# A ring of ten weight units instead of eight, residual rows parked in memory, and separate buffers for the last tiles, in a transformer block with a mixture of experts

## The chip, the cores and the metric

The kernel runs on one core of one Trainium2 chip. Its time is the device time of one execution in microseconds (us), the median of three runs. All work of the core is done by five engines with a program each: PE (matmul), DVE (vector), ACT (scalar activation), POOL (general) and SP (which here only issues transfers), and by 16 DMA engines that they share. Programs wait for each other by semaphores.

## The reference

One block over 1024 tokens of width 1024, all in fp32. A projection feeds two mixers (a chunked mLSTM and a sparse attention), their outputs go through `w_out`, and then come the residual and a mixture of experts, on which this change works:

```python
y = jnp.concatenate([y_m, y_n], axis=-1) @ w_out[l]
x = x + g_m * rms_norm(y, norm_mix_post[l])              # these are the "residual rows", x2 in the kernel
h = rms_norm(x, norm_ffn_pre[l]) * (1.0 + sc_f) + sh_f
y = hier_moe(h, router_grp_w[l], ..., expert_w1[l], expert_w3[l], expert_w2[l])
x = x + g_f * rms_norm(y, norm_ffn_post[l])

# hier_moe: each token picks one of 4 groups, then 2 of its 8 experts; for each block of rows of one expert
xb = hf[toks]
hb = jax.nn.silu(xb @ w1[ei]) * (xb @ w3[ei])            # w1, w3: 1024 x 512
return (hb @ w2[ei]) * gts[:, None]                      # w2: 512 x 1024
```

There are 32 experts, each with three weight matrices of 2048 KB, and 2048 pairs of a token and an expert.

## The kernel before

Everything on chip lies in one array, `arena`, of 53200 words in each of 128 partitions, which the program cuts into regions that later stages use again. The stages that matter here are the last four.

**Stage E** (from about 786 us) runs over 8 tiles of 128 tokens. For each tile PE turns the mixers' output and multiplies it with `w_out`, ACT and DVE normalise it, DVE adds the rows of `x` (loaded into `xt[t % 2]`) and writes the sum into `x2[:, t, :]`, which stays on chip in the region `QT` until the very end. The tile, normalised once more (`xn2`), is stored to `d_xn` in memory. After the last tile the router runs on DVE: it counts the rows of each expert, ranks the experts by that count and writes `row_tok` and `expert_at`, the tables that say which tokens and which expert stand at which place. The semaphore `table_ready` marks this.

**Places.** The experts are given 32 places. Places 0 to 2 belong to experts 0, 1 and 2 whatever their count, so that their weights can be loaded before the router is done; the others follow by falling count. The capacity falls with the place (`CAP_STEPS`): 128 rows at places 0 to 6, 96 at 7 to 13, 64 at 14 to 26, 32 at 27 to 31. What doesn't fit goes to extra blocks of 128 rows behind the 32 steps (`over_block`); with these inputs there is one.

**The expert stage** handles the places in the order of the list `ORDER`, one in each step q. PE does in a step: "up" (rows times w1 and w3, `f_up`), the turning of the next step's rows (`f_turn`), "down" of the step before (hidden times w2, `f_down`) and the turning of the hidden rows (`f_turn_hidden`). POOL gathers the rows of step q from `d_xn` two steps ahead, ACT and DVE do the gating, DVE copies the results out and ACT stores them to `d_y`. SP loads the weights: one unit is one matrix of 2048 KB, `(1, q)`, `(3, q)` or `(2, q)` for w1, w3 or w2 of step q, and there are eight slots for units (`SLOT`). `LOADS` is the order of the loads, the unit number v goes to slot v % 8, and it may start when unit v - 8 has been used (`slot_free`): w1 after the first half of "up" (semaphore `up_half`), w3 after the second (`up_done`), w2 after "down" (`down_done`). SP takes its instructions in order, so a load that waits holds back all that follow. The first eight units belong to places 0 to 2 and need no table.

**The final stage** starts when all results are stored (`stage_f`). POOL gathers for each of 8 tiles of 128 tokens the two experts' rows from `d_y` into `y1` and `y2`, ACT scales the first, DVE adds the second, ACT sums the squares, DVE normalises, scales and adds `x2[:, t, :]`, and SP stores the tile to `out`. `y1` and `y2` have four buffers each (`NG = 4`): from tile 4 on, POOL waits until the tile four before has been stored.

Of the kernel before, what the change touches and what calls it, by code (L numbers as in the profile page):

```python
# [85 lines left out]
def weight_loads():  # L86
# [7 lines left out]
LOADS = weight_loads()  # L94
# [65 lines left out]
def build(nc, d, out):  # L160
    JOB = job_list()
    ITEMS = ring_items(d)
    with ExitStack() as ctx:
# [162 lines left out]
        x2 = view(QT, NT, D)  # L326
# [47 lines left out]
        NG = 4  # L374
        y1 = [view(SLOT[0] + D * i, D) for i in range(NG)]
        y2 = [view(SLOT[0] + D * (NG + i), D) for i in range(NG)]
        junk_g = view(SLOT[0] + 2 * NG * D, D)
# [15 lines left out]
        w_in = [sem(f"w_in{j}") for j in range(8)]  # L393
# [11 lines left out]
        y_in = [sem(f"y_in{i}") for i in range(4)]  # L405
        g_scaled, g_added, g_sq, g_sqrt, g_done = (sem(n) for n in ("g_scaled", "g_added", "g_sq", "g_sqrt", "g_done"))
        out_stored = [sem(f"out_stored{i}") for i in range(4)]
# [143 lines left out]
        def _(sp):  # L551
# [101 lines left out]

            sp.wait_ge(x_sq, NT)
            sp.wait_ge(psum_ready, JOB[("xT2", NT - 1, 1)] + 1)
            for s in range(2):
                sp.wait_ge(xn_stored[s], 16 * NT // 2)
            load_static(5)
            sp.wait_ge(stage_end["E"], 4)
            sp.wait_ge(table_ready, 1)  # L660
            load_static(6)
            for v in range(8, len(LOADS)):
                n, q = LOADS[v]
                e = q
                if q >= 3:
                    e = sp.value_load(expert_at[ORDER[q]:ORDER[q] + 1, 0:1], min_val=0, max_val=NE - 1)
                slot_free(v - 8)
                load_weight(v % 8, n, e)

            def load_over(i, s):  # L670
# [18 lines left out]
            for t in range(NT):
                sp.wait_ge(g_done, t + 1)  # L690
                sp.dma_start(out[t * P:(t + 1) * P, :], y1[t % NG]).then_inc(out_stored[t % NG], 16)
            for s in range(NG):
                sp.wait_ge(out_stored[s], 16 * NT // NG)

        @block.gpsimd
        def _(pool):
# [103 lines left out]
            for t in range(NT):  # L800
                if t >= NG:
                    pool.wait_ge(out_stored[t % NG], 16 * (t // NG))
                for k, y in enumerate((y1, y2)):
                    pool.indirect_dma_start(y[t % NG], None, d_y,
                                            bass.IndirectOffsetOnAxis(ap=dest[:, k, t:t + 1], axis=0)).then_inc(y_in[t % NG], 16)
# [1281 lines left out]
```

## Time and profile before

| | |
|---|---|
| Time, median of 3 runs | 1637.09 us (1636.88 to 1637.14) |
| Time of the profiled execution | 1636.61 us |
| Its span | 1634.8 us |
| Granted TensorE clock, mean over the span | 0.924 of full |
| PE busy | 1360.1 us (83%) |
| DVE busy | 632.0 us (39%) |
| ACT busy | 385.1 us (24%) |
| Moved by DMA | 323.01 MB, mean 198 GB/s |

All times in the rows are microseconds from the start of the span unless marked ns. The profiled execution took 1.8 us more than its span, in what lies around it. "Busy" of PE counts matmuls, also those at the lower clock. In a row of the timeline the first number is the start and the second the duration of a merged group of instructions (merging can take in short waits between them); the bracket at its end is idle time of that engine just before, and what ended it. "DMA share" is the mean busy share of the 16 DMA engines.

### The profile page before, as it was taken

How to read it: one execution, taken by the hardware profiler on the slowest of the kernel's cores; microseconds unless marked ns; L12 is line 12 of the kernel's file. 1: busy time of each engine (PE TensorE's matmuls, PEld its weight loads, DVE VectorE, ACT ScalarE, POOL GpSimd, SP SyncE). 2: the span in 40 equal slices, each digit the busy share in tenths (PEclk: the TensorE clock that was granted, in tenths of full speed). 3: DMA queues.
4: the chain of work that ended last, by engine and by line, in shares of the span. 5: the costliest groups of instructions: out<-in, count | busy, mean ns of one | idle time of the engine just before them, and what ended most of it. 6: DMA issues, size and time to landing. Idle time of an engine off the chain costs nothing.

```text
span 1634.8 us, 17119 instructions
## 1 busy us (share of the span) xinstructions
PE 1360.1 (83%) x6271; PEld 693.1 (42%) x6271; DVE 632.0 (39%) x1400; ACT 385.1 (24%) x873; POOL 77.7 (5%) x109
## 2 busy tenths in 40 slices
PE   2899999999866889998899838999797897898730
PEld 2744444444664444444455424444343343343310
DVE  5626324502065666665333371223122122122216
ACT  2233311101185565544133300000000000000013
POOL 0000000000103000000000000000000000000012
PEclk8899999999997999999999958999899899999975
DMA  9612222202502930000421256699999999999835
GB/s 336 134 51 78 86 81 103 70 33 103 205 2 60 293 117 1 1 1 1 180 78 52 73 207 233 223 403 401 405 405 389 410 397 392 411 389 408 369 116 205
DMA packets 107771, 323.01 MB, mean 198 GB/s; under 512 B 26012, under 2 KB 50216, under 8 KB 99112
## 3 DMA queue, kind: packets, MB, share of 16 engines
q1 hardware_dynamic: 95192, 291.48, 47.6%
q0 software_dynamic: 5712, 19.42, 3.7%
q10 hardware_dynamic: 6784, 11.02, 1.8%
q8 instruction: 51, 0.84, 0.2%
q14 instruction: 32, 0.26, 0.0%
HBM read 283.59 MB, written 38.30 MB: 197 GB/s over the span
## 4 chain that ended last, share of the span: by engine, by line
PE 36%; DMA 13%; DVE 5%; issue 2%; SPq 2%; ACT 2%; POOL 0%; DVEq 0%; ACTq 0%; POOLq 0%
DMA arena<-expert_w 10%; PE ps L1444 7%; PE ps L1433 7%; PE ps L1393 6%; PE ps L1483 5%; PE ps L1299 2%; SPq L623 2%; PE ps L1316 2%; PE ps L1336 2%; ACT arena L980 1%; PE ps L1423 1%; DVE arena L1988 1%; PE ps L1378 1%; DMA d_y<-arena 1%; DMA arena<-d_y,arena 1%
## 5 line engine op out<-in xcount | busy, mean ns | idle before, releaser
L1444 PE MATMUL ps<-arena 128*32 128x256 f32 (+1 forms) x1408 | 203.5, 515 | 49.4 <-DMA arena<-expert_w 48.6
L1154 PE MATMUL ps<-arena 128*128 128x512 f32 x512 | 221.0, 593 | 0.0
L1483 PE MATMUL ps<-arena 128*32 128x256 f32 (+2 forms) x832 | 152.7, 498 | 6.6 <-issue 3.9
L1154 PEld LDWEIGHTS ps<-arena 128*128 128x128 f32 x512 | 97.1, 190 | 119.5 <-issue 119.4
L1444 PEld LDWEIGHTS ps<-arena 128*32 128x32 f32 (+1 forms) x1408 | 78.5, 131 | 160.6 <-issue 147.5
L1161 PE MATMUL ps<-arena 128*128 128x512 f32 (+1 forms) x384 | 142.0, 530 | 1.2 <-ACT arena L825 1.2
L1433 PE MATMUL ps<-arena 128*128 128x512 f32 x256 | 116.1, 612 | 12.9 <-DVE arena L1988 12.9
L1393 PE MATMUL ps<-arena 128*128 128x512 f32 x256 | 112.7, 593 | 0.1
L980 ACT ACTIVATE arena<-arena 128x640 f32<-128x640 f32 (+7 forms) x128 | 92.7, 726 | 59.2 <-DVE arena L1790 59.2
L1161 PEld LDWEIGHTS ps<-arena 128*128 128x128 f32 x384 | 72.5, 189 | 68.7 <-issue 62.0
L1046 ACT ACTIVATE arena<-ps 64x512 f32<-64x512 f32 x20 | 11.8, 589 | 365.3 <-PE ps L1444 365.3
L1316 PE MATMUL ps<-arena 128*128 128x128 f32 x528 | 80.2, 286 | 21.2 <-ACT arena L980 9.2
L1999 DVE TENSOR_TENSOR arena<-arena,ps 64x512 f32<-64x512 f32 x20 | 13.8, 690 | 214.5 <-ACT arena L1046 115.2
L1790 DVE CUSTOM_DVE_ANT_0 arena<-ps,arena 128x640 f32<-128x640 f32 (+7 forms) x128 | 84.5, 704 | 31.4 <-PE ps L1299 29.2
L1483 PEld LDWEIGHTS ps<-arena 128*32 128x32 f32 (+2 forms) x832 | 56.6, 132 | 82.1 <-issue 73.0
L1316 PEld LDWEIGHTS ps<-arena 128*128 128x128 f32 x528 | 58.6, 142 | 77.4 <-issue 25.3
L1299 PE MATMUL ps<-arena 64*128 64x512 f32 (+3 forms) x384 | 73.7, 499 | 14.6 <-DVEq L530 8.5
L1433 PEld LDWEIGHTS ps<-arena 128*128 128x128 f32 x256 | 49.5, 196 | 74.2 <-issue 66.3
L1988 DVE TENSOR_SCALAR arena<-ps,arena 128x64 f32<-128x64 f32 (+3 forms) x264 | 74.4, 356 | 10.0 <-PE ps L1423 8.0
L775 POOL DMA_INDIRECT arena<-d_xn,arena x32 | 30.0, 937 | 933.3 <-PE ps L1423 479.0
L1336 PE MATMUL ps<-arena 128*64 128x512 f32 x264 | 72.0, 625 | 0.0
L1393 PEld LDWEIGHTS ps<-arena 128*128 128x128 f32 x256 | 47.3, 189 | 54.7 <-issue 54.7
(318 smaller groups left out, 1312.4 us busy)
## 6 DMA issues: line engine op xcount, KB each, us to landing
arena<-expert_w SPq DMA_DIRECT2D x99, 2048.0 KB, 33.0
arena<-ada_w SPq DMA_DIRECT2D x12, 2048.0 KB, 9.2
d_y<-arena SPq DMA_DIRECT2D x24, 512.0 KB, 5.9
arena<-x SPq DMA_DIRECT2D x16, 512.0 KB, 4.0
arena<-w_in SPq DMA_DIRECT2D x4, 2048.0 KB, 12.9
d_y<-arena ACTq DMA_DIRECT2D x40, 128.0 KB, 7.9
arena<-w_out SPq DMA_DIRECT2D x2, 2048.0 KB, 14.0
d_xn<-arena SPq DMA_DIRECT2D x8, 512.0 KB, 2.6
```

What stands on the lines that cost most here:

```text
L980: nc.scalar.activation(p_, p_, ACT.Exp, scale=-1.0, bias=nmax[:, (u + g) % 8:(u + g) % 8 + 1], accum_out=sums[:, t % 2, "csw".index(kind), ...
L1154: last = nc.tensor.matmul(b, w(k), hT[:, k, 512 * c:512 * c + 512], start=(k == 0), stop=(k == KT - 1))
L1161: last = nc.tensor.matmul(b[:, 0:width], hT[:, k, P * t:P * t + P], w[:, k, at_col:at_col + width], start=(k == 0), stop=(k == KT - 1))
L1299: last = nc.tensor.matmul(b, qT[half, h, at_t], src[half, first + at_:first + at_ + w], start=True, stop=True)
L1316: last = nc.tensor.transpose(b[g][:, P * h:P * h + P], probs[kind][g][h][:, P * i:P * i + P], ident)
L1336: last = nc.tensor.matmul(ps[HD * g:HD * g + HD, 6, :], vv[:, blocks[i], P * k + HD * g:P * k + HD * g + HD], probs_T[q % 2][g], start=(i ...
L1393: last = nc.tensor.matmul(b, yT[t % 2][:, k, :], w[:, k, :], start=(k == 0), stop=(k == KT - 1))
L1433: last = nc.tensor.matmul(ps[:, 2 + n, :], xgT[s][:, k, :], w_up[slots[n]][:, k, :], start=(k == 0), stop=(k == KT - 1))
L1444: last = nc.tensor.matmul(ps[width * j:width * j + width, 2 if width == 64 else 3, 0:span], xgT[s][:, k, lo:lo + width], w_up[slots[n]][:, ...
L1483: last = nc.tensor.matmul(dst, hid_T[s][:, at_:at_ + width], w_down[slot][:, k, span * j:span * j + span], start=(k == 0), stop=(k == 3))
L1790: V.tensor_tensor_reduce(probs[kind][g][h][:, 0:n], ps[:, b0:b0 + 2, :].rearrange("p a n -> p (a n)")[:, 0:n] if n > 512 else ps[:, b0, 0: ...
L1988: last = V.tensor_scalar(xgT[s][:, k, 0:rows], turned_at(k, rows), scale_f[:, k:k + 1], shift_f[:, k:k + 1], ALU.mult, ALU.add)
```

## The change

Four things are changed, and they hang together by the room on chip.

- The residual rows no longer stay on chip. DVE adds in place in `xt[t % 2]`, SP stores that tile to a new memory tensor `d_x2`, and loads the next `x` tile into the buffer only when the store has landed. The region `QT` becomes two weight slots. All of `d_x2` is read back (two transfers of four tiles each) after the last "up" of the 32 steps, into the two slots of that step's w1 and w3.
- The ring has ten slots. Unit v (from 10 on) takes the slot of unit v - 10 in the order in which units are *used* (`USES`), not loaded.
- `ORDER` is changed: the three fixed experts (places 0, 1, 2) stand at steps 0, 2 and 4, and places 27, 28 and 29, of 32 rows, stand between them. All nine units of the fixed experts are loaded before the table is ready: five at the start of stage E, two at its next to last tile, two at its end.
- In the final stage each tile has its own `y1` and `y2`, and POOL no longer waits for stores of `out`.

```diff
-SLOT = [0, 4096, 8192, MQT, MKT, MKT + 4096, MKT + 8192, YM]
-ORDER = [0, 1, 2, 14, 27, 7, 3, 15, 8, 16, 28, 17, 4, 9, 18, 19, 29, 10, 20, 5, 21, 11, 30, 22, 23, 12, 6, 24, 25, 13, 26, 31]
+SLOT = [0, 4096, 8192, QT, QT + 4096, MQT, YM, MKT, MKT + 4096, MKT + 8192]
+NS = 10
+ORDER = [0, 27, 1, 28, 2, 29, 14, 7, 3, 30, 15, 8, 16, 17, 4, 9, 18, 19, 10, 20, 5, 21, 11, 22, 23, 12, 6, 24, 25, 13, 26, 31]
...
-    loads = [(n, q) for q in range(2) for n in (1, 3)] + [(2, 0), (2, 1), (1, 2), (3, 2)]
-    for q in range(3, NE):
-        loads += [(1, q), (3, q), (2, q - 1)]
-    return loads + [(2, NE - 1)]
+def weight_uses():
+    uses = []
+    for q in range(NE):
+        uses += [(1, q), (3, q)] + [(2, q - 1)] * (q > 0)
+    return uses + [(2, NE - 1)]
+USES = weight_uses()
+EARLY = [(n, q) for q in range(NE) if ORDER[q] < 3 for n in (1, 3, 2)]
+LOADS = EARLY + [u for u in USES if u not in EARLY]
+SLOT_OF, FILLS, fills = {}, {}, [0] * NS
+for v, u in enumerate(LOADS):
+    SLOT_OF[u] = v if v < NS else SLOT_OF[USES[v - NS]]
...
-        x2 = view(QT, NT, D)
-        NG = 4
+        NG = NT
+        x2_slots = [SLOT_OF[(n, NE - 1)] for n in (1, 3)]
+        x2_back = [view(SLOT[j], 4, D) for j in x2_slots]
...
-            for v in range(3):
+            for v in range(5):
                 load_static(v)
             for t in range(NT):
                 sp.wait_ge(x2_done, t + 1)
-                if t + 2 < NT:
-                    sp.dma_start(xt[t % 2], d["x"][(t + 2) * P:(t + 3) * P, :]).then_inc(xt_in[t % 2], 16)
-                if t == NT - 1:
-                    sp.wait_ge(psum_ready, JOB[("out", NT - 1, 1)] + 1)
-                    for v in (3, 4, 7):
-                        load_static(v)
+                sp.dma_start(d_x2[t * P:(t + 1) * P, :], xt[t % 2]).then_inc(x2_stored[t % 2], 16)
                 sp.wait_ge(xn2_done, t + 1)
                 sp.dma_start(d_xn[t * P:(t + 1) * P, :], xn2[t % 2]).then_inc(xn_stored[t % 2], 16)
+                if t + 2 < NT:
+                    sp.wait_ge(x2_stored[t % 2], 16 * (t // 2) + 16)
+                    sp.dma_start(xt[t % 2], d["x"][(t + 2) * P:(t + 3) * P, :]).then_inc(xt_in[t % 2], 16)
+                if t == NT - 2:
+                    sp.wait_ge(psum_ready, JOB[("yT", NT - 1, 1)] + 1)
+                    load_static(5)
+                    load_static(6)
...
+            for v in range(NS - 1, len(LOADS)):
                 n, q = LOADS[v]
+                if v >= NS:
+                    slot_free(USES[v - NS])
...
+            sp.wait_ge(up_done, NE)
+            for a in range(2):
+                sp.dma_start(x2_back[a], d_x2[4 * P * a:4 * P * a + 4 * P, :].rearrange("(t p) n -> p t n", p=P)).then_inc(x2_in, 16)
...
             for t in range(NT):
-                if t >= NG:
-                    pool.wait_ge(out_stored[t % NG], 16 * (t // NG))
...
-                V.tensor_tensor(x2[:, t, :], y_row, xt[t % 2], ALU.add).then_inc(x2_done, 1)
+                V.tensor_tensor(xt[t % 2], xt[t % 2], y_row, ALU.add).then_inc(x2_done, 1)
...
+            dve.wait_ge(x2_in, 32)
             add_experts(0)
```

PE at the start of the expert stage, before. L1433 is "up" of 128 rows, L1423 the turning of the next rows (the second number of its shape is how many), L1456 the turning of the hidden rows, L1483 "down", L1444 "up" of fewer rows.

```order
L1423 MATMUL ps<-arena 128x128 x8
L1433 MATMUL ps<-arena 128x512 x16
L1423 MATMUL ps<-arena 128x128 x8
L1456 MATMUL ps<-arena 128x128 x4
L1433 MATMUL ps<-arena 128x512 x16
L1423 MATMUL ps<-arena 128x128 x8
L1483 MATMUL ps<-arena 128x512 x8
L1456 MATMUL ps<-arena 128x128 x4
L1433 MATMUL ps<-arena 128x512 x16
```

The same place after the change, where these lines are L1451, L1441, L1474 and L1479, L1501 and L1462:

```order
L1441 MATMUL ps<-arena 128x128 x8
L1451 MATMUL ps<-arena 128x512 x16
L1441 MATMUL ps<-arena 128x32 x8
L1474 MATMUL ps<-arena 128x128 x4
L1462 MATMUL ps<-arena 32x256 x32
L1441 MATMUL ps<-arena 128x128 x8
L1501 MATMUL ps<-arena 128x512 x8
L1479 MATMUL ps<-arena 128x64 x2
L1451 MATMUL ps<-arena 128x512 x16
L1441 MATMUL ps<-arena 128x32 x8
L1501 MATMUL ps<-arena 32x256 x16
```

Three steps of 128 rows stood in a row; now a step of 32 rows follows each of them.

SP from the seventh tile of stage E to the first loads with the table, before. L646 loads `x`, L652 stores `xn2`, L623 loads w1 or w3 and L621 w2, L666 reads `expert_at`.

```order
L646 DMA arena<-x 128x1024 [waits x2_done]
L652 DMA d_xn<-arena 128x1024 [waits xn2_done]
L652 DMA d_xn<-arena 128x1024 [waits xn2_done,x2_done]
L623 DMA arena<-expert_w 128x4096 [waits psum_ready,x2_done]
L621 DMA arena<-expert_w 128x4x1024
L623 DMA arena<-expert_w 128x4096
L652 DMA d_xn<-arena 128x1024 [waits xn2_done]
L621 DMA arena<-expert_w 128x4x1024 [waits xn_stored0,xn_stored1,psum_ready,x_sq]
L623 DMA arena<-expert_w 128x4096 [waits table_ready,stage_endE]
L666 TENSOR_LOAD arena
```

And after the change (L660 stores `d_x2`, printed `d_x`; L662 stores `xn2`, L665 loads `x`, L637 and L635 load weights, L683 reads `expert_at`):

```order
L660 DMA d_x<-arena 128x1024 [waits x2_done]
L662 DMA d_xn<-arena 128x1024 [waits xn2_done]
L665 DMA arena<-x 128x1024 [waits x2_stored1]
L660 DMA d_x<-arena 128x1024 [waits x2_done]
L662 DMA d_xn<-arena 128x1024 [waits xn2_done]
L635 DMA arena<-expert_w 128x4x1024 [waits psum_ready]
L637 DMA arena<-expert_w 128x4096
L660 DMA d_x<-arena 128x1024 [waits x2_done]
L662 DMA d_xn<-arena 128x1024 [waits xn2_done]
L637 DMA arena<-expert_w 128x4096 [waits x2_stored1,x2_stored0,psum_ready]
L635 DMA arena<-expert_w 128x4x1024 [waits xn_stored1,xn_stored0]
L683 TENSOR_LOAD arena [waits table_ready,stage_endE]
```

A load of `x` now stands behind two stores and a wait, and no weight load but the tenth waits for the table.

## Rows read from the trace of the kernel before

**Rows 1.** The page: GB/s in the 40 equal slices of the span.
```profile
GB/s 336 134 51 78 86 81 103 70 33 103 205 2 60 293 117 1 1 1 1 180 78 52 73 207 233 223 403 401 405 405 389 410 397 392 411 389 408 369 116 205
```
**Rows 2.** Windows: stretch, its length, busy of each engine, PEclk, DMA share, GB/s.
```profile
955.00:977.00 22.00, 7.05 (x32) 6.90 (x32) 19.08 (x69) 0.00 (x0) 1.85 (x1) 0.50 0.27 96
977.00:1010.00 33.00, 23.76 (x61) 11.78 (x62) 6.88 (x20) 1.88 (x2) 2.83 (x3) 0.78 0.67 240
1010.00:1060.00 50.00, 50.00 (x155) 22.80 (x155) 11.26 (x27) 1.78 (x3) 2.68 (x3) 1.00 0.61 210
1060.00:1549.00 489.00, 425.67 (x2637) 186.21 (x2636) 118.49 (x323) 17.34 (x35) 23.80 (x28) 0.94 1.01 401
...
986.00:1537.00 551.00, 491.65 (x2828) 216.19 (x2828) 130.63 (x351) 21.01 (x40) 27.39 (x31) 0.95 0.96 376
```
**Rows 3.** Waits of PE from 1062 to 1545 us.
```profile
PE ps L1444 <- DMA arena<-expert_w: 48.6, 13, 7.7
```
**Rows 4.** Timeline of PE, expert stage, one row for each kind of work.
```profile
986.08 16.59 PE L1433 MATMUL ps<-arena 128*128 128x512 f32 x32 [2.81 <-DVE arena L1988]
...
1021.03 7.04 PE L1483 MATMUL ps<-arena 128*128 128x512 f32 x16
...
1028.35 13.92 PE L1433 MATMUL ps<-arena 128*128 128x512 f32 x32
...
1066.22 3.66 PE L1444 MATMUL ps<-arena 128*32 128x256 f32 x64
...
1086.43 1.94 PE L1483 MATMUL ps<-arena 128*32 128x256 f32 x32
```
**Rows 5.** Timeline of SP, first loads with the table.
```profile
996.01 7.18 SPq L623 DMA_DIRECT2D arena<-expert_w  x2
```
**Rows 6.** L623, all its loads.
```profile
DMA to landing us min/median/max: 8.1/33.6/41.2
```
**Rows 7.** The page: DMA issues, count, KB each, median us to landing.
```profile
arena<-expert_w SPq DMA_DIRECT2D x99, 2048.0 KB, 33.0
...
arena<-x SPq DMA_DIRECT2D x16, 512.0 KB, 4.0
...
d_xn<-arena SPq DMA_DIRECT2D x8, 512.0 KB, 2.6
```
**Rows 8.** Timeline, the end of the expert stage.
```profile
1535.44 1.93 PE L1483 MATMUL ps<-arena 128*32 128x256 f32 x32 [1.87 <-DMA arena<-expert_w]
...
1540.46 0.42 DVE L2017 COPY arena<-ps 128x256 f32<-128x256 f32 x1 [6.22 <-DMA d_y<-arena]
...
1544.66 15.49 PE L1433 MATMUL ps<-arena 128*128 128x512 f32 x32 [6.05 <-DVE arena L1988]
...
1571.14 1.18 ACTq L1058 DMA_DIRECT2D d_y<-arena  x2
...
1578.98 0.94 POOL L804 DMA_INDIRECT arena<-d_y,arena  x1 [70.76 <-DVEq L2048]
```
**Rows 9.** Windows, the final stage.
```profile
1579.00:1635.00 56.00, 0.00 (x0) 0.00 (x0) 31.22 (x32) 21.12 (x33) 17.99 (x16) 0.50 0.64 225
```
**Rows 10.** Waits in the final stage.
```profile
POOL arena L804 <- DMA out<-arena: 19.2, 4, 9.9
```
**Rows 11.** Timeline of the final stage, POOL, DVE and SP.
```profile
1580.23 0.94 POOL L804 DMA_INDIRECT arena<-d_y,arena  x1 [0.30 <-issue]
...
1594.01 1.23 DVE L2065 TENSOR_TENSOR arena<-arena 128x1024 f32<-128x1024 f32 x1
...
1630.41 1.23 DVE L2065 TENSOR_TENSOR arena<-arena 128x1024 f32<-128x1024 f32 x1
```
**Rows 12.** Timeline of SP, stage E.
```profile
832.24 0.33 SPq L646 DMA_DIRECT2D arena<-x  x1
834.90 0.33 SPq L652 DMA_DIRECT2D d_xn<-arena  x1
849.50 0.33 SPq L646 DMA_DIRECT2D arena<-x  x1
```

More of the change, by code:

```diff
@@ L83 @@
 STEP_ROWS = [rows_of(place) for place in ORDER]
-def weight_loads():
-    loads = [(n, q) for q in range(2) for n in (1, 3)] + [(2, 0), (2, 1), (1, 2), (3, 2)]
-    for q in range(3, NE):
-        loads += [(1, q), (3, q), (2, q - 1)]
-    return loads + [(2, NE - 1)]
-LOADS = weight_loads()
+def weight_uses():
[9 more added lines that the diff above has]
+    SLOT_OF[u] = v if v < NS else SLOT_OF[USES[v - NS]]
+    fills[SLOT_OF[u]] += 1
+    FILLS[u] = 16 * fills[SLOT_OF[u]]
+OVER_SLOT = [[SLOT_OF[USES[len(LOADS) - NS + 3 * s + j]] for j in range(3)] for s in range(2)]
+OVER_FILLS = [[16 * fills[j] for j in slots] for slots in OVER_SLOT]
 STORES = [0, 0]
@@ L372, in build @@
         assert small[0] <= late_end
-        NG = 4
-        y1 = [view(SLOT[0] + D * i, D) for i in range(NG)]
-        y2 = [view(SLOT[0] + D * (NG + i), D) for i in range(NG)]
-        junk_g = view(SLOT[0] + 2 * NG * D, D)
+        NG = NT
+        x2_slots = [SLOT_OF[(n, NE - 1)] for n in (1, 3)]
+        x2_back = [view(SLOT[j], 4, D) for j in x2_slots]
+        y_slots = [SLOT[j] for j in range(NS) if j not in x2_slots]
+        y1 = [view(y_slots[i // 4] + D * (i % 4), D) for i in range(NG)]
+        y2 = [view(y_slots[2 + i // 4] + D * (i % 4), D) for i in range(NG)]
+        junk_g = view(y_slots[4], D)
+        d_x2 = nc.dram_tensor("d_x2", (S, D), F32).ap()
         scale_f, shift_f = view(QT + 8192, KT), view(QT + 8200, KT)
@@ L392, in build @@
         exp_args, exps_done, hots_ready, slots_hot = sem("exp_args"), sem("exps_done"), sem("hots_ready"), sem("slots_hot")
-        w_in = [sem(f"w_in{j}") for j in range(8)]
+        w_in = [sem(f"w_in{j}") for j in range(NS)]
+        x2_stored, x2_in = [sem(f"x2_stored{i}") for i in range(2)], sem("x2_in")
         idx_ready = [sem(f"idx_ready{i}") for i in range(2)]
@@ L404, in build @@
         idx_seen, store_seen = sem("idx_seen"), sem("store_seen")
-        y_in = [sem(f"y_in{i}") for i in range(4)]
+        y_in = [sem(f"y_in{i}") for i in range(NT)]
         g_scaled, g_added, g_sq, g_sqrt, g_done = (sem(n) for n in ("g_scaled", "g_added", "g_sq", "g_sqrt", "g_done"))
-        out_stored = [sem(f"out_stored{i}") for i in range(4)]
+        out_stored = sem("out_stored")
         def key_blocks(t, kind):
@@ L688, in _ @@
                         load_over(i, 1)
+            sp.wait_ge(up_done, NE)
+            for a in range(2):
+                sp.dma_start(x2_back[a], d_x2[4 * P * a:4 * P * a + 4 * P, :].rearrange("(t p) n -> p t n", p=P)).then_inc(x2_in, 16)
             for t in range(NT):
                 sp.wait_ge(g_done, t + 1)
-                sp.dma_start(out[t * P:(t + 1) * P, :], y1[t % NG]).then_inc(out_stored[t % NG], 16)
-            for s in range(NG):
-                sp.wait_ge(out_stored[s], 16 * NT // NG)
+                sp.dma_start(out[t * P:(t + 1) * P, :], y1[t]).then_inc(out_stored, 16)
+            sp.wait_ge(out_stored, 16 * NT)
         @block.gpsimd
@@ L1512, in over_block @@
             def over_block(i, s):
-                q, loaded = 2 * i + NE + s, 16 * i + 16 * len(LOADS) // 8 + 16
+                q, slots = 2 * i + NE + s, OVER_SLOT[s]
+                loaded = [16 * i + 16 + n for n in OVER_FILLS[s]]
                 f_turn(q, s, P, i + NE // 2 + 1)
-                f_up(q, s, P, [3 * s, 3 * s + 1], [loaded, loaded])
+                f_up(q, s, P, slots[0:2], loaded[0:2])
                 f_turn_hidden(q, s, P)
-                f_down(q, s, P, 3 * s + 2, loaded)
+                f_down(q, s, P, slots[2], loaded[2])
             pe.wait_ge(table_ready, 1)
@@ L2064, in _ @@
                 link(V.scalar_tensor_tensor(a, a, rs, gf_row, ALU.mult, ALU.mult))
-                V.tensor_tensor(a, a, x2[:, t, :], ALU.add).then_inc(g_done, 1)
+                V.tensor_tensor(a, a, x2_back[t // 4][:, t % 4, :], ALU.add).then_inc(g_done, 1)
 def kernel(**inputs):
```

50 lines of the change are left out of this document (24 added, 26 removed).

## The prediction

> **What bounds the kernel now.** I read the page's slices first [rows 1]: from about 1060 us on (the 27th slice; each is 40.9 us) the DMA engines move some 400 GB/s in every slice until the experts are done, and nowhere else for so long. Then windows around that edge [rows 2]: 401 GB/s at a DMA share of 1.01 from 1060 to 1549 us, but 210 GB/s (0.61) from 1010 to 1060, 240 GB/s from 977 to 1010 and 96 GB/s in the 22 us before. So the expert stage has two halves: a short one in which the ring of slots starves the DMA engines, since PE spends 50.00 of 50 us busy on three experts of 128 rows and frees slots slowly, and a long one bound by the transfer of the weights. That PE is not the limit of the long half is seen in the waits: it waited 13 times, 48.6 us, for weights [rows 3], and from 986 to 1537 us its matmuls took 491.65 of 551 us, slower clock included [rows 2]; so PE alone could not end before 986 + 492 = 1478 us, some 59 us earlier than it did. In a stage bound by transfers the end moves by the bytes that are moved earlier, at 401 GB/s. After the stage come the extra block (to 1571 us) and the final stage (1579 us to the end) [rows 8, 9].
>
> **Term A, the ring and the order.** Two parts.
> First, more units are in place when the table is ready: nine instead of seven (before, the eighth is issued only with the table). The two are moved while the engines do 96 GB/s [rows 2]. 2 x 2.097 MB (2048.0 KB each [rows 7]) = 4.19 MB, at 401 GB/s 10.5 us.
> Second, the window from 1010 to 1060 us. Would the new ring keep the engines full there? Durations by shape [rows 4]: "up" of 128 rows 13.92 us, "down" 7.04; of 32 rows 3.66 and 1.94. Before, a step frees three units (6.29 MB) in 13.92 + 7.04 = 21.0 us of PE work, which can't feed more than 300 GB/s, less with the turnings between; the trace has 210. After, a pair of a large and a small step frees six units (12.6 MB) in 26.6 us, 473 GB/s, and still over 401 with some 3 us of turnings. I walked it through with these durations. PE begins at 986.08; half of step 0's "up" is done at about 995, and there the first freed slot gets (3,1), as the ring before did at 996.01 [rows 5]; alone it takes the shortest time from issue to landing, 8.1 us [rows 6], so it lands at 1004.1, 1.4 us after "up" of step 0 ends (986.08 + 16.59 = 1002.7). "Up" of step 1 ends at 1007.8 and frees two slots at once; the next are free at 1016 (down 0), 1023 and 1030 (up 2), 1033 (down 1), two at 1038 (up 3), 1046, 1053, 1060. The units queued one after another from 1008 on, at some 5.5 us each, would land at 1016, 21, 27, 32, 38, 43, 49, 54, 60: each slot is free before the unit ahead has landed. So from about 1010 us the queue is never empty. Regained: (401 - 210) x 50 us = 9.55 MB, 23.8 us.
> I take off 2 us for the start of the full rate (a transfer issued at 1008 delivers its first bytes later, and the row for 977 to 1010 stays as it is, since the ring is then full as before). A = -(10.5 + 23.8 - 2.0) = -32.3 us, for the landing of the last unit of step 31 and with it for its "down" (before at 1535.44 [rows 8]). The last seven steps are the same places in the same order, so the end of the stage keeps its shape. Bounds: at best -40 (no loss at the start, and some of the 240 GB/s window filled as well), at worst half of the second part is lost again, -20.
> The HBM Reference of the Trainium skill (section "Specifications (TRN2)") gives a core an effective share of about 358 GB/s of its memory stack. By that figure 13.7 MB would be worth 38.4 us rather than 34.3. The row of this kernel, which runs alone, has 401 GB/s over 489 us [rows 2], so I go by the row.
> For a single transfer DMA: Bandwidth & Descriptors of the Trainium skill (section "Anatomy of one DMA") gives about 2.0 us plus the bytes over 436 GB/s, as an estimate 6.8 us for a unit; (3,1) would then land at 1002.8, and PE would not wait for it. The row's shortest is 8.1; between the two lies 1 us.
>
> **Term B, the final tiles.** Before, the stage takes from POOL's first gather at 1578.98 to the end of the span at 1634.8, 55.8 us [rows 8, 9], of which POOL waited 19.2 us in four waits for stores of `out` [rows 10]; DVE is busy 31.22 us in it [rows 9], 3.9 us a tile. With own buffers POOL issues all 16 gathers at intervals of 1.25 us (1578.98, 1580.23 [rows 8, 11]), the last at 1597.7. What is late next? The transfers: 8 tiles of 1.05 MB gathered and, before the last has landed, four or five of 0.52 MB stored, 10.5 to 11 MB; the stage moves 225 GB/s at a share of 0.64 [rows 9], so 350 GB/s when full: 31 us, to about 1612. DVE: its first tile is done at 1594.01 + 1.23 = 1595.24 [rows 11], seven more at 3.9 us each give 1622.5. The DVE is the later, so the last tile ends at 1622.5 instead of 1630.41 + 1.23 = 1631.64: B = -9.1 us. Bounds: -12 (DVE without its 0.3 us between tiles and a quicker first one) and -3 (gathers and stores mix badly and DVE waits for most tiles as now).
>
> **Term C, the residual rows through memory.** Storing a tile to `d_x2`: 0.52 MB, like `d_xn`'s 2.6 us to landing [rows 7]. The load of `x` for tile t + 2 was issued at the end of the DVE add (832.24) and is now issued when the store has landed, some 3 us later. It takes 4.0 us [rows 7] and is needed two tiles on; a tile takes 849.50 - 832.24 = 17.26 us [rows 12], so there is over 25 us of room: nothing. Queued behind that wait on SP are the next stores only; the store of `xn2` now goes ahead of the load. The five early units take 5 x 5.2 = 26 us from the start of stage E at 786 and end at about 812, before the first store (832.24 - 17.26 = 815). Two more, issued when tile 6 is through, take 10.5 us and end within the 17.26 us to tile 7's stores (832.24 + 6 x 17.26 = 936). The read-back of 4.19 MB, 10.5 us at 401 GB/s, is issued behind the last weight load, while PE still has the extra block's 15.49 us of "up" and its "down" before it, and DVE needs it only in the final stage: cover of some 30 us. If that cover were gone it would cost 10.5 us. C = 0, between 0 and +4 (the read-back runs beside the stores of steps 30 and 31, of which DVE waited for one for 6.22 us already [rows 8]).
> In-place adding and the ring's new bookkeeping cost nothing: same instructions on DVE, and on SP only constants changed.
>
> **Sum.** 1636.61 - 32.3 - 9.1 + 0 = 1595.2 us for the profiled execution; the median of the runs lay 0.5 us above it, so 1595.7 us.
>
> **Rivals.**
> 1. *The ring is only half as good* (14%). SP takes its loads in order, and one late "down" holds back several free slots; or rows gathered late make PE slip while slots are few. For it: 210 GB/s in the window before came from just such waits. Against: my walk has 4 to 10 us of spare at each load. It gives A = -20, B = -9: 1608 us.
> 2. *The final stage gains little* (9%). All 16 gathers and the stores of `out` share engines; if stores then take 6 us and DVE waits for tiles as before, B = -3: 1602 us. Against: the share is 0.64 now.
> 3. *Better than the sum* (7%). PE waits less, so fewer matmuls run at the lower clock level (1.2 GHz) which followed its idle times (mean granted clock 0.94 of 2.4 GHz from 1060 us on [rows 2]), and the 977 to 1010 window fills too: A = -40, B = -11: 1586 us.
> 4. *The other side, slower* (3%). One mechanism: the load of `x` behind the store of the same buffer. Loads 5 to 7 queued with it in stage E, or a store that lands late behind weights (a weight unit waits 33.0 us to land in a full queue [rows 7]), delay the add of a tile. It decides once a load is over 25 us late, and it must be so for the six reloaded tiles by 7 us each beyond that to eat the 41 us: 1640 us. Against: no weight is in the queue from tile 0 to tile 5.
> 5. *It does nothing for the transfers* (2%): were the queue bound by something that grows with the units outstanding, A would be 0 to -5 and B is left, with C's 4 us: about 1632 us, or no change.
> The forecast itself has 65%, with its own range of 1588 to 1603 us.
>
> **How the numbers follow.** Rival 1 lies just inside 1612, rival 3 inside 1584, which leaves out rivals 4 and 5 and the tails of the others: 1584 to 1612 us for 8 in 10. A measurement of this kernel can tell 0.2%, 3.3 us. Faster by more than that are the forecast, 1, 2, 3 and half of 5: 0.96; within it half of 5: 0.01; slower: rival 4: 0.03.
>
> **What would show it right or wrong.** In the new profile: windows from 1010 to 1060 us at about 400 GB/s rather than 210; PE's "up" of step 2 starting near 1016, step 4 near 1046; full rate ending near 1517 for the weights, with 10 us of reading rows behind it; PE's waits for weights shorter in sum than 48.6 us, but still there, since transfers bound the stage; stage E and the table at the same times as before (977 us); no wait of POOL in the final stage, and that stage 46 to 47 us long. The prediction is wrong if the window at 1010 stays under 300 GB/s, if the table is ready later, or if PE rather than DMA ends the stage.

## The result, and the profile after

| | before | after |
|---|---|---|
| Time, median of 4 runs | 1636.99 us | 1597.11 us (1597.0 to 1597.23) |
| Profiled execution, span | 1636.61, 1634.8 us | 1597.23, 1595.4 us |
| Mean granted TensorE clock | 0.924 | 0.930 |
| Moved by DMA | 323.01 MB | 331.40 MB |

The ratio after to before is 0.9761 (95% interval 0.9749 to 0.9773): 39.9 us less, where 41 were forecast. The rows are read in the order of the prediction. First the page's slices, as in [rows 1]: the plateau begins in the 26th slice instead of the 27th. The 38th is its last in both, but a slice is 39.9 us here and was 40.9, so it ends at about 1516 us instead of 1553.

```profile
GB/s 337 144 53 54 93 106 105 53 53 106 123 89 5 236 240 1 1 1 1 124 245 79 79 263 96 365 391 401 382 399 393 410 395 394 392 393 405 418 193 290
```

The windows that answer to [rows 2] (stretch, length, busy of PE, of its weight loads PEld, of DVE, ACT, POOL, granted clock, DMA share, GB/s):

```profile
955.00:977.00 22.00, 7.04 (x32) 6.90 (x32) 18.19 (x68) 0.00 (x0) 2.74 (x2) 0.50 0.04 7
977.00:1010.00 33.00, 26.62 (x125) 13.47 (x126) 6.19 (x19) 2.26 (x3) 1.82 (x2) 0.75 0.64 226
1010.00:1060.00 50.00, 50.00 (x218) 23.26 (x216) 12.20 (x32) 1.57 (x3) 2.74 (x3) 1.00 1.01 396
1060.00:1500.00 440.00, 407.14 (x2448) 174.46 (x2446) 113.78 (x304) 16.91 (x34) 23.95 (x27) 0.97 1.02 397
```

From 1010 to 1060 us the engines now move 396 GB/s instead of 210; before 977 they stand almost still (7 GB/s), since all nine fixed units are in. From 977 to 1010 us the rate is 226 GB/s, before 240: the prediction had left that window as it was. The long half moves 397 GB/s, a little less than the 401 of before. PE at the start of the stage (start, duration, what; compare [rows 4]):

```profile
983.98 16.95 PE L1451 MATMUL ps<-arena 128*128 128x512 f32 x32 [2.81 <-DVE arena L2006]
...
1003.85 5.19 PE L1462 MATMUL ps<-arena 128*32 128x256 f32 x64 [1.35 <-DVE arena L2006]
...
1017.20 14.03 PE L1451 MATMUL ps<-arena 128*128 128x512 f32 x32
...
1034.60 3.66 PE L1462 MATMUL ps<-arena 128*32 128x256 f32 x64
...
1046.43 14.03 PE L1451 MATMUL ps<-arena 128*128 128x512 f32 x32
```

The walk had steps 2 and 4 begin near 1016 and 1046; they begin at 1017.20 and 1046.43. PE waits for weights 31.8 us in place of 48.6 [rows 3]:

```profile
PE ps L1462 <- DMA arena<-expert_w: 31.8, 10, 5.4
```

The end of the stage, as in [rows 8]:

```profile
1507.34 1.93 PE L1501 MATMUL ps<-arena 128*32 128x256 f32 x32 [1.62 <-DMA arena<-expert_w]
...
1511.45 0.42 DVE L2035 COPY arena<-ps 128x256 f32<-128x256 f32 x1 [5.07 <-DMA d_y<-arena]
...
1515.64 15.66 PE L1451 MATMUL ps<-arena 128*128 128x512 f32 x32 [5.14 <-DVE arena L2006]
...
1550.15 0.94 POOL L822 DMA_INDIRECT arena<-d_y,arena  x1 [70.48 <-DVEq L2066]
```

"Down" of step 31 comes 28.1 us earlier (1535.44 to 1507.34), the first gather of the final stage 28.8 us earlier. In that stage the four waits of POOL for stores [rows 10] are gone, and DVE's last add ends at 1592.36:

```profile
1565.40 1.22 DVE L2084 TENSOR_TENSOR arena<-arena 128x1024 f32<-128x1024 f32 x1
...
1569.24 1.22 DVE L2084 TENSOR_TENSOR arena<-arena 128x1024 f32<-128x1024 f32 x1
...
1591.14 1.22 DVE L2084 TENSOR_TENSOR arena<-arena 128x1024 f32<-128x1024 f32 x1
```

The stage takes 1595.4 - 1550.15 = 45.25 us instead of 55.8, that is 10.6 less. 28.8 + 10.6 = 39.4 us, the whole difference of the two profiled executions (1636.61 - 1597.23). In the repeat of the changed kernel (e11 below) step 31's "down" starts at 1504.67, 2.7 us earlier than here, and ends at 1508.25, 1.0 us earlier; the first gather starts at 1549.29, 0.9 us earlier. Differences of that size at these two places show nothing. Stage E and the table are in place as before: SP's first load with the table is issued at 977.21 after and with the table at 977.45 before.

### The profile page after: what moved, and what is told of

It reads as the page before. It is cut to its first block, busy times and chain, and to the rows that moved or that the text cites. A ratio compares the mean times of both kernels' runs of the same rounds, so it can differ in the third digit from the quotient of the medians.

```text
span 1595.4 us, 17126 instructions
## 1 busy us (share of the span) xinstructions
PE 1356.9 (85%) x6271; PEld 689.7 (43%) x6271; DVE 631.6 (40%) x1400; ACT 385.7 (24%) x873; POOL 76.5 (5%) x109
## 2 busy tenths in 40 slices
DMA packets 109979, 331.40 MB, mean 208 GB/s; under 512 B 26172, under 2 KB 50376, under 8 KB 101320
## 3 DMA queue, kind: packets, MB, share of 16 engines
q0 software_dynamic: 5712, 19.42, 3.6%
## 4 chain that ended last, share of the span: by engine, by line
PE 28%; SPq 17%; DVE 6%; DMA 4%; issue 2%; ACT 2%; DVEq 0%; POOL 0%; ACTq 0%
SPq L637 14%; PE ps L1411 6%; PE ps L1451 5%; PE ps L1501 4%; PE ps L1462 3%; DMA arena<-expert_w 2%; PE ps L1317 2%; PE ps L1334 2%; PE ps L1354 2%; SPq L635 2%; SPq L683 1%; ACT arena L998 1%; PE ps L1396 1%; PE ps L1441 1%; DMA d_y<-arena 1%
## 5 line engine op out<-in xcount | busy, mean ns | idle before, releaser
L1462 PE MATMUL ps<-arena 128*32 128x256 f32 (+1 forms) x1408 | 198.4, 501 | 34.1 <-DMA arena<-expert_w 31.8
L1501 PE MATMUL ps<-arena 128*32 128x256 f32 (+2 forms) x832 | 152.7, 498 | 4.3 <-issue 1.9
L1172 PEld LDWEIGHTS ps<-arena 128*128 128x128 f32 x512 | 96.9, 190 | 119.7 <-issue 119.6
L1462 PEld LDWEIGHTS ps<-arena 128*32 128x32 f32 (+1 forms) x1408 | 74.9, 127 | 143.6 <-issue 126.6
L1451 PE MATMUL ps<-arena 128*128 128x512 f32 x256 | 116.7, 614 | 7.9 <-DVE arena L2006 7.9
L1179 PEld LDWEIGHTS ps<-arena 128*128 128x128 f32 x384 | 72.3, 189 | 68.9 <-issue 62.1
L1334 PEld LDWEIGHTS ps<-arena 128*128 128x128 f32 x528 | 58.4, 141 | 77.5 <-issue 25.3
L1501 PEld LDWEIGHTS ps<-arena 128*32 128x32 f32 (+2 forms) x832 | 56.3, 132 | 80.1 <-issue 69.2
L1451 PEld LDWEIGHTS ps<-arena 128*128 128x128 f32 x256 | 49.6, 196 | 69.5 <-issue 65.9
L507 DVE COPY arena<-ps 128x512 f32<-128x512 f32 x66 | 45.7, 692 | 63.8 <-PE ps L1334 63.6
## 6 DMA issues: line engine op xcount, KB each, us to landing
arena<-expert_w SPq DMA_DIRECT2D x99, 2048.0 KB, 35.4
arena<-w_in SPq DMA_DIRECT2D x4, 2048.0 KB, 12.9
```

The lines of the kernel that those rows point to most:

```text
L1172: last = nc.tensor.matmul(b, w(k), hT[:, k, 512 * c:512 * c + 512], start=(k == 0), stop=(k == KT - 1))
L1179: last = nc.tensor.matmul(b[:, 0:width], hT[:, k, P * t:P * t + P], w[:, k, at_col:at_col + width], start=(k == 0), stop=(k == KT - 1))
L1334: last = nc.tensor.transpose(b[g][:, P * h:P * h + P], probs[kind][g][h][:, P * i:P * i + P], ident)
L1451: last = nc.tensor.matmul(ps[:, 2 + n, :], xgT[s][:, k, :], w_up[slots[n]][:, k, :], start=(k == 0), stop=(k == KT - 1))
L1462: last = nc.tensor.matmul(ps[width * j:width * j + width, 2 if width == 64 else 3, 0:span], xgT[s][:, k, lo:lo + width], w_up[slots[n]][:, ...
L1501: last = nc.tensor.matmul(dst, hid_T[s][:, at_:at_ + width], w_down[slot][:, k, span * j:span * j + span], start=(k == 0), stop=(k == 3))
```

## The experiments

The medians stand beside the median of the kernel before in the same session (1637.52, 1637.62 and 1636.35 us in the three sessions).

**e1_final: own buffers for the final tiles, nothing else.** In the kernel before:

```diff
-        NG = 4
...
-        y2 = [view(SLOT[0] + D * (NG + i), D) for i in range(NG)]
...
+        NG = NT
...
+        y2 = [view(SLOT[2 + i // 4] + D * (i % 4), D) for i in range(NG)]
...
-                if t >= NG:
-                    pool.wait_ge(out_stored[t % NG], 16 * (t // NG))
```

> The kernel before with the final tiles' own buffers alone (ring of eight, old order, residual rows on chip). My theory: the final stage is paced by DVE at 3.85 us a tile, as after the change (45.25 us from the first gather to the end of the span, before 55.8), and nothing ahead of it moves: 1637 - 10.6 = 1626.4 us. Rival: part of the 10.6 us came from elsewhere (the read-back rows, or an earlier start of the stage), and this gives 1630 us or more.

1625.38 us (before 1637.52), ratio 0.9915 (0.9898 to 0.9931). In its profile "down" of step 31 stands at 1536.02 and the first gather at 1578.34, both within 0.7 us of before, and the span ends at 1623.9: 45.6 us. Term B is worth 10 to 12 us by itself, without the ring, the order or the trip through memory.

**e2_x2mem: the residual rows through memory, nothing else.**

```diff
-                V.tensor_tensor(x2[:, t, :], y_row, xt[t % 2], ALU.add).then_inc(x2_done, 1)
+                V.tensor_tensor(xt[t % 2], xt[t % 2], y_row, ALU.add).then_inc(x2_done, 1)
...
+                sp.dma_start(d_x2[t * P:(t + 1) * P, :], xt[t % 2]).then_inc(x2_stored[t % 2], 16)
...
+                sp.dma_start(x2[:, 4 * a:4 * a + 4, :], d_x2[4 * P * a:4 * P * a + 4 * P, :].rearrange("(t p) n -> p t n", p=P)).then_inc(x2_in, 16)
```

> The kernel before with the residual rows through memory alone: stored to memory, the load of x behind that store, read back into their old region behind the last weights (one weight unit is loaded some 6 us later in stage E, since the tile buffer it overwrites is read longer). My theory: no cost, 1637 us, within 1 us; the load of x has over 25 us of room and the read-back of 10.5 us is covered by the extra block. Rival: the read-back delays stores and the end of the expert stage: 1639 to 1647 us.

1636.14 us (before 1637.52), ratio 0.9987 (0.9977 to 0.9996): the trip of 8.4 MB costs nothing. "Down" of step 31 is at 1535.75, the first final gather at 1578.47.

**e3_old_order: ten slots, old order.**

```diff
-ORDER = [0, 27, 1, 28, 2, 29, 14, 7, 3, 30, ...
+ORDER = [0, 1, 2, 14, 27, 7, 3, 15, 8, 16, ...
```

> The changed kernel with the old order of places (three fixed experts of 128 rows first), ring of ten kept. My theory: the ring starves again between 1010 and 1060 us, but later and less, since nine units are in place and ten slots give one step more; walking the frees, about 12 us of the gain go: 1609 us, the window from 1010 to 1060 us at about 300 GB/s. Rival: ten slots alone bring it all (1597 us, about 400 GB/s in the window); other rival: the order alone does, and this falls back to 1626 us.

1607.2 us, ratio 0.9808 (0.9791 to 0.9824), "down" of step 31 at 1515.76. Its window:

```profile
1010.00:1060.00 50.00, 50.00 (x155) 22.80 (x154) 11.75 (x29) 1.78 (x3) 2.74 (x3) 1.00 0.86 293
```

As expected, 293 GB/s: the slots alone do a little under half of the filling (210, 293, 396), and three steps of 128 rows in a row still starve the ring.

**e4_eight: eight slots, new order.**

```diff
-SLOT = [0, 4096, 8192, QT, QT + 4096, MQT, YM, MKT, MKT + 4096, MKT + 8192]
-NS = 10
+SLOT = [0, 4096, 8192, MQT, YM, MKT, MKT + 4096, MKT + 8192]
+NS = 8
...
-EARLY = [(n, q) for q in range(NE) if ORDER[q] < 3 for n in (1, 3, 2)]
+EARLY = [(n, q) for q in range(NE) if ORDER[q] < 2 for n in (1, 3, 2)]
```

> The changed kernel with eight slots (six fixed units loaded ahead, the rest with the table; the read-back goes into the region of the two missing slots), new order kept. My theory: the small steps free slots in time, but two slots fewer let the queue run dry now and then at the start: about 8 us lost, 1605 us; the rate in the long half goes up to 398 to 401 GB/s whatever the depth. Rival 1: the order alone brings it all, 1597 us. Rival 2 (a deeper queue of weights slows the DMA engines): the long half then runs faster than with ten slots, by 3 GB/s or 3 to 4 us, and that makes up for half of the loss: 1601 us.

1605.96 us, ratio 0.9805 (0.9789 to 0.9821), "down" of step 31 at 1514.68. The time is as expected, the reason is not:

```profile
977.00:1010.00 33.00, 25.49 (x126) 13.34 (x127) 6.65 (x21) 2.26 (x3) 2.23 (x4) 0.79 0.81 298
1010.00:1060.00 50.00, 50.00 (x218) 23.21 (x216) 11.83 (x32) 1.57 (x3) 2.50 (x3) 1.00 1.00 404
1060.00:1500.00 440.00, 404.11 (x2344) 171.34 (x2345) 112.40 (x302) 16.83 (x33) 23.88 (x27) 0.96 1.02 398
```

With eight slots the queue does not run dry from 1010 us on; I had expected that it would. The loss is only that six units instead of nine are in place at 977 us, partly made up by the two slots filled at that moment. The depth of the queue does not set the rate: 398 GB/s here, 397 with ten slots, and 400 with ten slots in the old order (e3, same stretch). The same window of the changed kernel's repeats has 399 and 400 (e11, e10), so the rival's 3 GB/s between eight and ten slots would be no more than the scatter, and they don't show: the eight slots lie inside it. The queue is not much deeper, though. A weight unit took 31.2 us to land in the median with eight slots and 35.4 with ten, about an eighth more, so a rate that falls in a much deeper queue is not tested.

**e9_six_ahead: ten slots, new order, six units ahead.** The line of `EARLY` as in e4, ten slots kept.

> The changed kernel (ten slots, new order) with only the six units of the first two fixed experts loaded ahead of the table; four free slots are filled when the table is ready. My theory: what counts is the bytes moved before the stream is full, wherever they go: with four free slots the DMA engines are full from 977 us, about 370 to 400 GB/s in the window 977 to 1010 instead of 226 (5 to 5.7 MB more), against 6.3 MB fewer ahead: 1 to 3 us lost, 1599 us. Rival: the third expert's early load is what the two slots are worth, and this equals the kernel with eight slots, 1606 us; other rival: the queue so filled delays the first gathers, 1602 us or more.

1599.08 us (ratio 0.9775, 0.9760 to 0.9790); the changed kernel in the same session 1596.15 (0.9742, 0.9726 to 0.9758): 2.9 us lost, where 1 to 3 were expected. The windows 977 to 1010 and 1010 to 1060:

```profile
977.00:1010.00 33.00, 26.01 (x127) 13.48 (x128) 7.22 (x23) 2.26 (x3) 2.61 (x3) 0.80 0.99 391
1010.00:1060.00 50.00, 50.00 (x222) 23.55 (x220) 11.82 (x31) 1.57 (x3) 1.94 (x3) 1.00 1.02 404
```

The engines are full from the moment of the table, and "down" of step 31 is at 1505.92, between the two traces of the changed kernel (1504.67, 1507.34). A unit loaded ahead and a unit loaded at 391 instead of 226 GB/s a moment later are worth nearly the same.

**e6_few_rows: what the gathered rows cost.**

```diff
-                rows, place = STEP_ROWS[q], ORDER[q]
+                rows, place = STEP_ROWS[q] if q == 0 else P if q == 1 else 32, ORDER[q]
```

> The changed kernel in which the gathers of steps 2 to 31 bring only 32 rows each (left out: the other rows of these steps, whose place in the buffer keeps old rows; step 1 gathers 128 instead of 32). 1440 rows or 5.9 MB less, weights, matmuls and stores as they were. My theory: rows cost the DMA engines more than their bytes (from the two traces: what the full-rate time holds beyond weights at 429 GB/s is some 34 ns for each row gathered and stored, so 17 ns a row), which is why the long half moved 398 and not 401 GB/s: 20 to 25 us less, 1572 to 1577 us, with over 405 GB/s from 1060 to 1480 us. Rival: rows cost only their bytes: 5.9 MB at 398 GB/s, 15 us less, 1582 us, rate unchanged.

1570.67 us (before 1637.62), 26.4 us below the changed kernel's 1597.11; "down" of step 31 at 1481.07, 26.3 us earlier than in the profile above.

```profile
1481.07 1.94 PE L1501 MATMUL ps<-arena 128*32 128x256 f32 x32 [1.22 <-DMA arena<-expert_w]
...
1060.00:1480.00 420.00, 404.01 (x2457) 173.12 (x2456) 113.83 (x305) 17.20 (x34) 22.57 (x27) 0.98 1.02 408
```

The expectation counted 1440 rows, but step 1 gathers 96 more: the page's queue of the gathers has 5712 packets and 19.42 MB in the changed kernel and 4368 and 13.91 MB here, that is 1344 rows and 5.5 MB less. 26.3 us for 1344 rows of 4 KB are 19.6 ns a row, or 209 GB/s; against the repeat of the changed kernel (1504.67) they are 23.6 us, 17.6 ns and 233 GB/s. By their bytes at 398 GB/s it would have been 14 us, so the rival is out for either trace. The rate of the rest rises to 408 GB/s.

**e8_half_w2: how far PE is from being the limit.**

```diff
-                    sp.dma_start(w_down[j], src.rearrange("a (k p) n -> p (a k) n", p=P)).then_inc(w_in[j], 16)
+                    sp.dma_start(w_down[j][:, 0:2, :], src.rearrange("a (k p) n -> p (a k) n", p=P)[:, 0:2, :]).then_inc(w_in[j], 16)
...
-                            last = nc.tensor.matmul(dst, hid_T[s][:, at_:at_ + width], w_down[slot][:, k, span * j:span * j + span],
+                            last = nc.tensor.matmul(dst, hid_T[s][:, at_:at_ + width], w_down[slot][:, k % 2, span * j:span * j + span],
```

> The changed kernel with only half of each w2 transferred (left out: its second 256 rows; down uses the first half twice, so PE's work is the same). 34.6 MB less, 87 us of transfers. My theory: DMA ends the expert stage now and PE is next, with a margin of the some 36 us that it waits: PE never waits for weights, down of step 31 near 1473 us instead of 1507.3, total 1561 us. Rival: PE is held by the chain through ACT and DVE within each step, and less than 25 us come, 1572 us or more.

1552.29 us (2 runs), 44.8 us below the changed kernel; I had put 36. PE's waits for weights are gone:

```profile
1060.00:1480.00 420.00, 415.20 (x2530) 176.81 (x2529) 118.12 (x316) 17.79 (x35) 23.87 (x27) 0.99 0.98 376
```

In the timeline of PE (start, duration, what) the extra block's "up" follows:

```profile
1467.65 16.83 PE L1451 MATMUL ps<-arena 128*128 128x512 f32 x32 [3.08 <-DVE arena L2006]
```

It starts at 1467.65 instead of 1515.64, 48 us earlier. 31.8 us of that are the waits of the changed kernel for weights. The rest goes with a higher granted clock (0.99 of full here, 0.97 there) and some shorter waits; the two are not taken apart. So transfers end the stage, and PE is the next limit, some 45 us off. The DMA share doesn't tell this: it is still 0.98, at 376 GB/s, in a stage in which PE is busy for 415.20 of 420 us and never waits for weights.

**e5a_table and e5b_pool: the final stage.** The first adds one square root on ACT before it waits for the gathers, the second also gives POOL the last add of tiles 2 to 7:

```diff
+            nc.scalar.activation(sum_g[:, 0:1], eps_col, ACT.Sqrt)
```
```diff
-                V.tensor_tensor(a, a, x2_back[t // 4][:, t % 4, :], ALU.add).then_inc(g_done, 1)
+                if t < 2:
+                    dve.wait_ge(g_norm, t + 1)
+                    V.tensor_tensor(a, a, x2_back[t // 4][:, t % 4, :], ALU.add).then_inc(g_done, 1)
...
+            for t in range(2, NT):
+                pool.wait_ge(g_norm, t + 1)
+                nc.gpsimd.tensor_tensor(y1[t], y1[t], x2_back[t // 4][:, t % 4, :], ALU.add).then_inc(g_done, 1)
```

> The changed kernel with one more small square root on ACT while it waits for the first gathered tile, so that the table load of 1.28 us is done ahead. My theory: the final stage is a chain from the first tile on and then DVE at 3.85 us a tile, so what the first tile gains the end gains: 1.3 us less, 1595.8 us. Rival: the later gathers pace the stage, and nothing moves: 1597.1 us.

1595.0 us (1591.09 to 1596.11), ratio to before 0.9732 (0.9717 to 0.9747). By the medians this is not told from the changed kernel's repeat (0.9742, 0.9726 to 0.9758). In the profile the stage takes 1593.8 - 1549.65 = 44.15 us, 1.1 less than 45.25, and the repeat has 45.2 (1594.5 - 1549.29): the gain of the first tile reaches the end.

> As the one with the early table, and the last add (residual rows) of tiles 2 to 7 moved from DVE to POOL. My theory: DVE falls to 2.7 us a tile, and then the transfers pace the stage (12.6 MB at 380 to 400 GB/s, from 1551 us to 1583) with the last tile's chain behind them: 5 to 7 us less than the changed kernel, 1590 to 1592 us. Rival: POOL needs over 4 us for an add of 128 x 1024 words, or slows DVE while it runs, and the stage gets no shorter or longer: 1597 us or more.

1600.12 us, ratio 0.9766 (0.9752 to 0.9780), 5 us above e5a: the rival. The timeline of both engines, two tiles apart:

```profile
1570.81 1.28 DVE L2090 SCALAR_TENSOR_TENSOR arena<-arena 128x1024 f32<-128x1024 f32 x1
...
1572.27 2.87 POOL L829 TENSOR_TENSOR arena<-arena 128x1024 f32<-128x1024 f32 x1 [0.72 <-DVE arena L2090]
...
1573.39 2.83 DVE L2090 SCALAR_TENSOR_TENSOR arena<-arena 128x1024 f32<-128x1024 f32 x1
...
1589.40 2.34 POOL L829 TENSOR_TENSOR arena<-arena 128x1024 f32<-128x1024 f32 x1 [1.16 <-DVE arena L2090]
...
1589.43 3.39 DVE L2090 SCALAR_TENSOR_TENSOR arena<-arena 128x1024 f32<-128x1024 f32 x1
...
1592.90 2.34 POOL L829 TENSOR_TENSOR arena<-arena 128x1024 f32<-128x1024 f32 x1 [1.16 <-DVE arena L2090]
```

The same DVE operation takes 1.28 us without POOL's add and 2.83 to 3.39 beside it; the add takes 2.34 to 3.33. The 1.55 us that DVE's operation grows by at the least are more than the 1.22 us of the add that it is rid of. In all five tiles it ends 1.07 to 1.09 us after POOL's add ends (1573.39 + 2.83 against 1572.27 + 2.87, 1589.43 + 3.39 against 1589.40 + 2.34). That looks like waiting for POOL and then running, rather than like running slowly; no run tests it.

**e10_tail and e11_after_again.** The early square root, and on DVE the evacuation of the extra block's rows ahead of the copy of step 31; beside it the changed kernel once more.

```diff
+            with dve.If(NE < v_blocks):
+                f_turned(NE, 0, P)
             static_result(NE - 1)
```

> The changed kernel with the early table on ACT, and with DVE's evacuation of the extra block's turned rows placed ahead of its copy of step 31's result, which waited 5.07 us for a store. My theory: the extra block's up starts 2.5 us earlier and is then held by its weights (the last of w3 lands at about 1519 us), 2.5 us less than the kernel with the early table alone: 1592.5 us. Rival: w1 and w3 of the extra block land no earlier than PE needs them, or the copy's store then ends later, and nothing is gained: 1595 us.

> The changed kernel again, beside the one with the reordered tail, so that both are compared on one chip: 1597 us, within 2 us.

1592.84 us (1589.01 to 1595.57), ratio 0.9731 (0.9716 to 0.9745), and 1596.15 us (1590.40 to 1596.38), ratio 0.9742 (0.9726 to 0.9758). The intervals overlap, so e10_tail is the lowest median but not shown to be faster. Its profile says why little came from the reordering:

```profile
1511.91 17.02 PE L1452 MATMUL ps<-arena 128*128 128x512 f32 x32 [2.82 <-DVE arena L2007]
...
1531.32 8.84 PE L1502 MATMUL ps<-arena 128*128 128x512 f32 x16 [0.87 <-DVE arena L2028]
...
1549.56 0.94 POOL L822 DMA_INDIRECT arena<-d_y,arena  x1 [71.06 <-DVEq L2072]
```

"Up" starts 2.6 us before that of the changed kernel beside it (1514.49), but takes 17.02 us instead of 15.95, and "down" 8.84 instead of 7.15; the final stage starts at 1549.56, there at 1549.29. The longer "down" runs at the lower level of the clock (1.2 GHz) for part of its time: from 1530 to 1535 us the granted clock is 0.67 here and 1.00 in e11. What stays of the gain in the profile is the table's microsecond. Both profiled executions are the slowest of their five, so what made 1589.01 or 1590.40 us of others is open.

## Why the prediction was right, and where its terms were off

**Bound and mechanism (right).** None of the prediction's three signs of being wrong shows: the window at 1010 has 396 GB/s, the table stands at 977.21, and the last "down" still waits for its weights (1.62 us). The stage was bound by transfers, and the small steps between the fixed experts fill the window from 1010 us. e3 and e4 show that either part alone brings about 20 of the 28 us (1515.76 and 1514.68 for "down" of step 31 against 1535.44 and 1507.34): the two overlap, since both fill the same gap. The prediction did not say that. That the ring of eight is not dry from 1010 us in the new order was not foreseen either; the two slots pay by units in place ahead of the table, or filled at it (e9). The bound that PE alone could not end before 1478 us was too late: with the waits gone, "down" of step 31 starts at 1461.46 in e8. It had counted 491.65 us of matmuls at a mean granted clock of 0.95; e8 has 472.25 us at 0.99 from 986 to 1462 us. Nothing hung on the bound.

**The total (1595.7, measured 1597.11).** It is closer than its terms: up to the first gather 3.5 us less were gained than forecast, in the final stage 1.5 us more. That the two errors have opposite signs is luck.

**Term A (-32.3, measured -28.1 at step 31, -28.8 at the first gather).** The bytes were right (12.9 MB, with the 2 us taken off; measured 13.0), their price was not. Up to 1060 us each kernel has moved, in MB from the windows, the units ahead (2.097 each) + 33 us x first rate + 50 us x second rate (e3's first rate is 243 GB/s, e11's two are 228 and 395):

| | slots, order, units ahead | MB by 1060 us | down of step 31 | us per MB more |
|---|---|---|---|---|
| before | 8, old, 7 | 33.1 | 1535.44 | |
| e3 | 10, old, 9 | 41.5 | 1515.76 | 2.3 |
| e4 | 8, new, 6 | 42.6 | 1514.68 | 2.2 |
| e9 | 10, new, 6 | 45.7 | 1505.92 | 2.3 |
| after | 10, new, 9 | 46.1 | 1507.34 | 2.2 |
| e11, the same | 10, new, 9 | 46.1 | 1504.67 | 2.4 |

The prediction took 2.49 us per MB, the mean rate of 401 GB/s, and none of these kernels gained as much per MB. That mean holds gathered and stored rows too, whose number does not change; the gathered ones cost as much as 209 to 233 GB/s would (e6), the stored ones were not measured. What is brought forward is weights, and these go at the rate of a stretch with hardly anything else, in stage E of the changed kernel:

```profile
800.00:810.00 10.00, 10.00 (x31) 4.83 (x30) 0.00 (x0) 1.42 (x3) 0.00 (x0) 1.00 1.04 433
```

433 GB/s are 2.31 us per MB, and the 10 us before this window, at 417 GB/s, 2.40: 13.0 MB are 30.0 to 31.2 us instead of 32.4. The mis-sized step is the conversion of bytes into time by the mixed rate, 1.2 to 2.4 us. That the row's price is what separates 2.49 from the measured 2.2 to 2.4 is argued from e6 and this window; no run changes it alone. The rest is not settled and lies within the scatter: the changed kernel's "down" of step 31 starts at 1504.67 to 1507.34 in four traces with the same work up to there (e5a, e5b and e11 are the others), 28.1 to 30.8 us earlier than before, and its first gather at 1549.29 to 1550.54, 28.4 to 29.7 us earlier.

The 358 GB/s of the Trainium skill's HBM Reference (section "Specifications (TRN2)"), which the prediction set aside, is by that section the share of a core while both cores of a pair stream; alone it gives a core about 425. This kernel runs on one core, and its rows lie above the share and near the second figure: 391 to 433 GB/s in the full windows shown here. The 6.8 us for one unit that the prediction worked out of the Trainium skill's DMA: Bandwidth & Descriptors (section "Anatomy of one DMA") rest on a fit for transfers that POOL issues; SP issues these, and the shortest took 8.1 us in both profiles.

**Term B (-9.1, measured -10.6; e1: -12.1 in the median, -10.3 in the profile).** DVE does pace the stage: 3.85 us a tile by the rows above (1565.40, 1569.24), and the gathers are never late after the second tile. The first tile ended 16.5 us after the first gather, where the trace of before had 16.3. Mis-sized were the seven intervals after it, for which I took DVE's 31.22 us over 8 tiles, 3.9 each. Six of them are 3.85, which is 0.3 us in all; the last is 2.65, since no add of a next tile stands in it, and that is the other 1.25 us.

**Term C (0).** Right, and shown alone by e2. The load of `x` is issued about 3 us after the add (818.25 after 815.22) and DVE never waits for it; the read-back is issued at 1514.25, lands within 19.4 us and is in well before the final stage at 1550.15.

**The rivals.** Rival 1 (the ring half as good) would have shown under 300 GB/s from 1010 us; it is what e3 does with the old order. Rival 2 (the final stage gains little) is refuted by e1. Rival 3 (better than the sum) came true in part: the granted clock from 1060 us on rose from 0.94 to 0.97 and B was 10.6 of its 11 us, but the window from 977 to 1010 did not fill (226 GB/s) and A stayed 9 us or more short of its 40. Rival 4 (slower, by the load behind the store) is refuted by e2. Rival 5 (the change does nothing for the transfers) is refuted by A itself, and e4 beside the changed kernel shows no rate that falls with two slots more.

## What to carry to other kernels

Where a stage is bound by transfers, count the bytes that a change brings forward and look at what frees the buffers: small work between large work filled this ring as well as two more slots did (20.8 and 19.7 us), and doing both does not add up (28 to 31). Price the bytes by the rate of the traffic that moves, not by the mean rate of a mixed stretch, whose slow part stays. A DMA share near 1 doesn't say that transfers end a stage: look whether the compute engine still waits for them (e8).
Give each late tile its own buffer when a store stands between it and its reuse; after that the engine with the most work per tile sets the pace, and handing part of it to an engine that slows it down is no relief.

## What the runs showed of the hardware that was not expected

- A gathered row of 4 KB cost the DMA engines 17.6 to 19.6 ns in a full queue (e6: 23.6 to 26.3 us for 1344 rows), as much as 7.6 to 8.5 KB of weights at 433 GB/s.
- DVE's second `scalar_tensor_tensor` on a tile (128 x 1024 words) took 1.28 us without and 2.83 to 3.39 us beside a POOL `tensor_tensor` of the same size, and ended 1.07 to 1.09 us after it each time (e5b). The POOL operation took 2.34 us, or 2.87 to 3.33 where it started while DVE's first one (1.27 to 1.28 us) ran. POOL's issue of gathers beside DVE did not slow DVE: 1.28 to 1.29 us in all rows of the changed kernel.
- The rate of the long stretch (1060 to 1500 us) was the same with eight and with ten slots: 398 and 401 GB/s with eight (e4, before), 397 to 400 with ten (the changed kernel, e3, e9, e11).
- The DMA share stayed at 0.98 while the engines moved 376 GB/s and PE waited for no weights (e8); in the stretches that transfers bound it was 1.02 at 397 to 408 GB/s.
